# Decoder step on one core: the output projection of two prompt tiles moved between the last value products of attention, one tile left in the mixer, and evictions moved up in their steps

## The reference

```python
q_r, k_r, v_r, g_r, q_a, k_a, v_a = project(hp, w_in[i], pos_p)
ret_o, ret_fin = retention_prompt(q_r, k_r, v_r)
att_o = dilated_attention_prompt(q_a, k_a, v_a)
mix = merge_heads(ret_o, g_r, att_o, w_out[i])       # concat([retention, attention]) @ w_out, 1024 x 1024
...
h1 = layer_norm(ALPHA * h + mix, ln1_g, ln1_b)
f, conv_state = conv_ffn(h1, prefix, w_up, conv_w, conv_b, w_down)
e = jax.nn.sigmoid(h1 @ w_ple_gate) * (p @ w_ple_proj)
return layer_norm(ALPHA * h1 + f + e, ln2_g, ln2_b), conv_state
```

## Time and profile before

| | us |
|---|---|
| median of 3 runs | 1517.49 (1517.3 to 1518.66) |
| the profiled execution | 1514.99 |
| its span | 1513.2 |
| TensorE busy in the span | 1384.5 (91%) |
| VectorE busy | 798.9 (53%) |
| ScalarE busy | 462.4 (31%) |
| GpSimd busy | 273.4 (18%) |
| mean granted clock of TensorE | 0.978 of full speed |

### The profile page before, as it was taken

One profiled execution on the slowest core, in us unless ns is written; L12 is line 12 of the kernel. 1 busy time (PEld: TensorE's weight loads), 2 busy tenths in 40 slices (PEclk: granted clock), 3 DMA queues, 4 the chain that ended last, 5 costly groups with the idle time before them and its releaser, 6 DMA issues. The chain is left out here.

```text
span 1513.2 us, 23893 instructions
## 1 busy us (share of the span) xinstructions
PE 1384.5 (91%) x8896; PEld 785.1 (52%) x8896; DVE 798.9 (53%) x1601; ACT 462.4 (31%) x753; POOL 273.4 (18%) x329
## 2 busy tenths in 40 slices
PE   2699999979999858999989999999999999999986
PEld 1355555545555433344536664466654666546642
DVE  8566766637667648385524543244431445314457
ACT  3322212227566620041113442034320343202322
POOL 6301010123433306022200110001010010100117
PEclk9999999989999979999999999999999999999998
DMA  7101111027587779350024121022210122101002
GB/s 230 42 29 42 34 38 33 11 66 139 118 158 151 146 171 292 127 173 8 8 58 130 55 82 42 0 62 62 83 42 0 47 77 83 42 0 42 15 14 105
DMA packets 184493, 115.76 MB, mean 76 GB/s; under 512 B 83319, under 2 KB 168263, under 8 KB 184151
## 3 DMA queue, kind: packets, MB, share of 16 engines
q1 hardware_dynamic: 184415, 114.73, 28.8%
HBM read 85.85 MB, written 10.15 MB: 63 GB/s over the span
## 5 line engine op out<-in xcount | busy, mean ns | idle before, releaser
L1731 PE MATMUL PS<-all_HT,all_WS 128*128 128x344 f16 x3168 | 465.4, 310 | 6.6 <-POOLq L73 4.8
L1731 PEld LDWEIGHTS PS<-all_HT,all_WS 128*128 128x128 f16 x3168 | 310.5, 98 | 162.1 <-issue 8.4
L1741 PE MATMUL PS<-all_WS,ffn_HG 128*128 128x512 f16 x608 | 182.4, 379 | 3.6 <-POOL ffn_HG L1891 1.9
L461 PE MATMUL PS<-all_WS,all_HT 128*128 128x512 f16 x768 | 174.9, 386 | 6.1 <-POOLq L73 6.1
L1891 POOL TENSOR_TENSOR ffn_HG<-ffn_PRD,ffn_HG 128x1032 f32 (+1 forms) x22 | 47.2, 2145 | 653.6 <-ACT ffn_HG L1863 653.6
L1851 ACT ACTIVATE ffn_C<-PS,all_CW,all_CWS 128x1032 f32<-128x1032 f32 x44 | 53.0, 1205 | 362.0 <-PE PS L1731 362.0
L818 PE MATMUL PS<-all_WS,all_HT 128*128 128x384 f16 x768 | 132.8, 331 | 3.6 <-POOLq L73 3.6
L461 PEld LDWEIGHTS PS<-all_WS,all_HT 128*128 128x128 f16 x768 | 75.9, 99 | 96.2 <-issue 8.2
L1741 PE MATMUL PS<-ffn_WD,ffn_HG 128*128 128x512 f16 x304 | 115.3, 379 | 0.0
L818 PEld LDWEIGHTS PS<-all_WS,all_HT 128*128 128x128 f16 x768 | 73.5, 99 | 55.0 <-POOLq L73 3.9
L1741 PEld LDWEIGHTS PS<-all_WS,ffn_HG 128*128 (+1 forms) x608 | 59.4, 98 | 76.9 <-issue 6.0
(11 more groups left out here) (230 smaller groups left out, 1860.7 us busy)
## 6 DMA issues: line engine op xcount, KB each, us to landing
ffn_SU<-in_w_up SPq DMA_DIRECT2D x42, 512.0 KB, 5.0
ffn_SD<-in_w_down SPq DMA_DIRECT2D x22, 512.0 KB, 3.5
all_STG<-in_w_in SPq DMA_DIRECT2D x32, 256.0 KB, 3.4
all_STG<-in_w_in SPq DMA_DIRECT2D x32, 192.0 KB, 3.3
samples_KC<-in_cache_k_win SPq DMA_DIRECT2D x24, 256.0 KB, 4.6
all_HRES<-in_x_prompt SPq DMA_DIRECT2D x8, 512.0 KB, 8.1
out<-attention_QKV SPq DMA_DIRECT2D x64, 64.0 KB, 1.7
all_STG<-in_w_out SPq DMA_DIRECT2D x8, 512.0 KB, 4.2
```

Source lines behind the costliest of these rows:

```text
L461: mm = nc.tensor.matmul(Z(p, s)[:n], HT[:, a, k, s * P:s * P + n], WS[:, slot, b, k, :], start=(k == 0 and (a, b) == (0, 0)), stop=(k == K ...
L1731: mm = nc.tensor.matmul(U(x)[:, third], UW[:, u, a, k, x * P:(x + 1) * P], HT[:, b, k, third * T3:(third + 1) * T3], start=(k == 0 and (a, ...
L1741: mm = nc.tensor.matmul(DB[u][:rows, half], HG[:, a, l, ds(t * P, rows)], WD[b][:, l, half * 512:(half + 1) * 512], start=(l == 0 and (a, ...
```

## The change

- Retention, TensorE: in step s = 8 the product that adds up the sample parts stands ahead of the transposition of `R` instead of behind it.
- Attention, TensorE: after the values of steps 36, 37, 38 and 39 stands `mix_half(t, half)`, the output projection of tile 0 (two halves of the contraction, 24 matmuls each) and tile 1. It takes the banks of `Z` and of the first head's scores, waits for their readers, for the split chunks of w_out (4 or 8 of them) and, in the second half, for the eviction of q = 3.
- Attention, ScalarE and VectorE: `out` goes to the head of ScalarE's step, and on VectorE behind the first `mask` of the step.
- Samples: `add(0)` and `add(1)` stand first on VectorE; TensorE does tiles 2 to 5, then the halves of tile 6; nothing stands around `weigh(1)` any more. The adds in the loop move from b = 2, 4, 6 to b = 3, 5, 7.
- Mixer: `mix` of tile 7 and the sample rows only; `gate(0)` goes chunk by chunk and waits for each chunk; ScalarE and VectorE have their splits in another order around the first tile.

```diff
@@ retention, TensorE
+                            if s == NT:
+                                pe.wait_ge(zp_ready, BASE + p + 1)
+                                nc.tensor.matmul(Z(p, s)[:NB], SUMS[:], ZP[:], start=True, stop=True).then_inc(z_ready, 1)
                             q, t = tile_at(s, 4, p, kind)
                             if t is not None:
                                 pe.wait_ge(r_ready, BASE + 8 * q + t + 1)
                                 pe.wait_ge(rlo, BASE + 8 * q + t)
                                 nc.tensor.transpose(RB, R[:, t % 2], IDENT[:]).then_inc(r_turned, 1)
-                            if s == NT:
-                                pe.wait_ge(zp_ready, BASE + p + 1)
-                                nc.tensor.matmul(Z(p, s)[:NB], SUMS[:], ZP[:], start=True, stop=True).then_inc(z_ready, 1)
@@ attention, TensorE
+                    def mix_half(t, half):
+
+                        if t == 0:
+                            pe.wait_ge(copied, BASE + NG)
+                        else:
+                            pe.wait_ge(masked, BASE + 2 * NA)
+                        pe.wait_ge(w_free, BASE + 2 + 4 * (HP - 1) + 4 * half + 4)
+                        if half:
+                            pe.wait_ge(mlo, BASE + (NA - NT) // 4 + 1)
+                        for c in range(2):
+                            for k in range(4 * half, 4 * half + 4):
+                                for a, b in PASSES:
+                                    nc.tensor.matmul(M[t][:, c], MT[:, a, k, t * P:(t + 1) * P], WS[:, k // 4, b, 2 * (k % 4) + c],
+                                                     start=(k == 0 and (a, b) == (0, 0)), stop=(k == KD - 1 and (a, b) == (1, 0)))
...
                         values(g - LP)
+                        if NG <= g < NG + 4:
+                            mix_half((g - NG) // 2, (g - NG) % 2)
@@ attention, ScalarE
                     for g in range(NG + LP + 2):
+                        out(g - LP - 1)
                         soften(g)
                         copy_sum(g - 1)
                         split(g)
-                        out(g - LP - 1)
@@ samples
-        EARLY = 6
+        DRAIN, EARLY = 2, 7
...
+                    add(0)
+                    add(1)
                     nc.vector.memset(OPS[0], 0.0).then_inc(bank_zero, 1)
                     for b in range(NB):
-                        if b in (2, 4, 6):
-                            add((b - 2) // 2)
+                        if b in (3, 5, 7):
+                            add(DRAIN + (b - 3) // 2)
...
-                    for t in range(4):
+                    for t in range(DRAIN, EARLY - 1):
                         mix(t)
...
                     weigh(0)
-                    mix(5, (0,))
                     weigh(1)
-                    mix(5, (1,))
@@ mixer, TensorE, gate(0) and the head of the stage
+                            pe.wait_ge(r_ready, BASE + 2)
+                            for k in range(KD):
+                                pe.wait_ge(wlo, BASE + k + 1)
...
-                    mix(0, 0, P, EARLY * P)
-                    mix(1, 1, P, (EARLY + 1) * P)
-                    pe.wait_ge(r_ready, BASE + 1)
+                    mix_product(0, P, EARLY * P).then_inc(mixed, 1)
@@ mixer, VectorE
                     add_mix(0, 0, P, EARLY)
-                    for c in range(4, KD):
-                        split(c)
+                    split(4)
                     low(0)
-                    add_mix(1, 1, P, EARLY + 1)
+                    split(5)
+                    add_mix(1, 1, NB, NT)
+                    split(6)
+                    split(7)
                     low_p(0)
-                    add_mix(2, 0, NB, NT)
```

More of the change, by code:

```diff
@@ L1200, in _ @@
                     then(nc.vector.tensor_scalar(SR[:R8, PAT * P:], MX[:R8, 1:2], LOG3, None, ALU.add))
-                    add(3)
+                    add(5)
                     dve.wait_ge(s_turned, BASE + 1)
@@ L1212, in _ @@
                     nc.vector.memset(OPS[1], 0.0).then_inc(bank_zero, 1)
-                    add(4)
+                    add(6)
                     dve.wait_ge(summed, BASE + 1)
@@ L1233, in _ @@
                                                        ALU.add).then_inc(att_done, 1)
-                    add(5)
                     dve.wait_ge(mhi, BASE + 4)
@@ L1257, in mix @@
                     def mix(t, halves=(0, 1)):
-                        if t >= 2 and 0 in halves:
+                        if 0 in halves:
                             pe.wait_ge(r_ready, BASE + t - 1)
@@ L1283, in _ @@
                     mm.then_inc(s_turned, 1)
-                    mix(4, (0,))
+                    mix(EARLY - 1, (0,))
                     pe.wait_ge(sr_ready, BASE + 2)
@@ L1398, in gate @@
                             pe.wait_ge(sig_ready, BASE + t)
+                        else:
+                            pe.wait_ge(r_ready, BASE + 2)
+                            for k in range(KD):
+                                pe.wait_ge(wlo, BASE + k + 1)
+                                for c in range(2):
+                                    for a, b in PASSES:
+                                        mm = nc.tensor.matmul(GB[:, c], HT[:, a, k, 0:P], WG[:, b, k, c * 512:(c + 1) * 512],
+                                                              start=(k == 0 and (a, b) == (0, 0)), stop=(k == KD - 1 and (a, b) == (1, 0)))
+                            mm.then_inc(gated, 1)
+                            return
                         for c in range(2):
@@ L1484, in copy_parts @@
                         nc.scalar.activation(PP[:], src.rearrange("p b n -> p (b n)"), ACT.Copy).then_inc(pp_ready, 1)
-                    for c in range(KD):
+                    for c in range(5):
                         split(c)
-                    copy_parts(M[0], 1)
+                    copy_parts(M[1], 1)
                     high(0)
+                    for c in range(5, KD):
+                        split(c)
                     high_p(0)
```

17 lines of the change are left out of this document (5 added, 12 removed).

## The result

The changed kernel takes 1511.57 us in the median of 20 runs (1508.55 to 1518.97), against 1518.73 for the kernel before, run 20 times beside it (1517.09 to 1523.52). The ratio is 0.9952, 95% interval 0.9944 to 0.9961: 7.2 us or 0.5% faster. The forecast was 14.2 us, its range ended at 1511.0: the direction was right, the size half of what was foretold.

A forecast was written before the change was run, and what follows sets the result against it. TensorE was busy 1384.5 of 1513.2 us, so only its idle time and lower-clock matmuls could be won. Terms 4.1 + 3.6 - 6.3 + 9.9 + 2.9 = 14.2 us less gave 1503.3 us, range 1498.8 to 1511.0.

The forecast's parts named there:

- Retention, 4.1 us less: Retention seams: the sum fits into the wait for R, 0.95 us at three seams, plus 1.26 for a slow projection.
- Attention, three head pairs, 3.6 us less: Attention's head-pair seams: sooner evictions of OB save 1.2 of a 1.71 us wait at each of three.
- the prediction's own sign of being wrong: Attention: the wait for probabilities grows by what the eviction's wait lost; the other sign was halves beyond 30 us in all.
- the seams give their gain back: Rival, retention and attention: the next waits end at the old time, 7.7 us lost, 1511.0 us; chance 0.13.
- End of attention, 6.3 us more: End of attention: four halves, one behind 3.9 us of idleness at the lower clock; samples begins at 562.7 instead of 556.43.
- The barrier: Between attention's last half and the start of samples: allowed 0.4 us.
- each half tile starts cold: Rival, end of attention: every half begins at the lower clock, 4.4 us more, 1507.7 us; chance 0.16.
- Samples, 9.9 us less: Samples: 5.3 us between the weigh calls, 3.3 behind weigh(1), 1.9 from the clock staying up, less 0.6 for an add.
- The add ahead of b = 3: Samples, VectorE: free if b = 3's multiplication waits for GpSimd's; costs 1.2 us if the two merely slow each other.
- Mixer, 2.9 us less: Mixer: gate(0) may start at 662.5, after the sample add_mix, instead of 665.36; bounds 0 and 3.5 us.
- The forecast case: Whole kernel: 14.2 us less, 1503.3 us, own range 1499 to 1507; chance 0.60.
- Faster: Whole kernel: measurably faster than before, where 3.0 us tells it from no change; chance 0.91.

The follow-up runs named there:

- run 20: Not a run label but a count: the kernel before was run 20 times beside the changed kernel; median 1518.73 us.
- e2_soon: The kernel before with only the evictions of OB moved up in their steps; 1520.11 us, ratio 1.0011.
- e6_loads: The changed kernel with attention's projection-weight loads and their splits moved out of steps s = 0 and 2; 1505.51 us, ratio 0.9915.
- e9_loads_only: The kernel before with only attention's projection-weight loads and their splits moved out of steps s = 0 and 2; 1513.93 us, ratio 0.9960.
- e10_loads_late: The changed kernel with loads and splits moved, first halves before second halves, and evictions of OB back at the end of their steps; 1505.81 us, ratio 0.9900.
- e11_keys: The changed kernel with loads moved, first halves before second halves, and keys of sample rows 2 and 3 loaded ahead of the retention state; 1500.38 us, ratio 0.9860.
- e1_zsum: The kernel before with only the retention part: the sample-part sum ahead of the transposition of R; 1512.90 us, ratio 0.9955.
- e4_order: The changed kernel with first halves of both tiles before the second halves at the end of attention; 1505.15 us, ratio 0.9906.
- e5_order_late: The changed kernel with first halves before second halves and evictions of OB back at the end of their steps; 1509.02 us, ratio 0.9940.
- e7_order_loads: The changed kernel with first halves before second halves and attention's projection-weight loads and splits moved; 1499.28 us, ratio 0.9874.

## Why the prediction was wrong in size

**Retention, 4.1 us less: right, a little small.** The stage lost 4.6 us (mean of three without the edit 256.2, of eleven with it 251.6), the time 5.9. A seam gave 1.05 to 1.4 us instead of 0.95: the projection follows the transposition after 0.17 us where it took 1.21, and from the projection behind one seam to that behind the next it took 58.99 and 59.02 us instead of 60.04 and 60.45. The slow projection behind the third seam took 6.33 to 6.63 us in the three kernels without this part and 5.34 in all eleven with it. Seams and projection together gave 5.3 us, of which 0.8 is lost again between the last transposition and attention.

**Attention, three head pairs, 3.6 us less: the step that failed.** "What is late next is the transposed probabilities", I wrote, and took 1.2 of 1.71 us all the same. Measured: nothing in the time (e2_soon), and in after the waits for the eviction (5.1 us in the head pairs) came back as waits for probabilities, 10.2 us instead of 3.7: the prediction's own sign of being wrong. The stage took 200.2 to 201.4 us with late evictions and 198.5 to 204.8 with sooner ones. It was the rival "the seams give their gain back", for this half. I had given it 0.13, arguing that VectorE's work starts sooner too. It did, by 1.4 us at the first seam, but between VectorE and the values stands SyncE's queue, whose rows I had not read, and it issued the transposition no sooner (18.95 to 19.07 us into the step, with late evictions and with sooner ones, but for e2_soon). e6_loads and e9_loads_only show that loads and splits were in the way, by the profile mostly through the queue; e10_loads_late shows that moving them does not free the seams' gain: about 1.4 of the 1.78 us per seam stay lost, and how much of that is still the queue no run here separates.

**End of attention, 6.3 us more: mechanism right, 3.9 us too small.** The end took 48.1 to 49.3 us in the four kernels with this order and sooner evictions, against 38.5 to 39.0. In after, measured from the last projection's start at 518.72, the last values' half ends 45.8 us later where I had 44.3: the chunks came 1.3 us later than forecast (25.5 instead of 24.2), and a first half of 6.05 us was not fully at 2.4 GHz. The barrier I had put at 0.4 us; it takes 2.32, of which 1.68 stood in the earlier trace rows for all to read. The first product of before waited for no semaphore of its stage; now it waits for `add(0)`, and so also until GpSimd has added BASE (line 73, the releaser that the profile names). `add(0)` itself was done 0.8 us before the product began. The earlier trace rows put the fall of the clock at 541.1 rather than 541.6, which changes nothing in the sum. The rival "each half tile starts cold" did not come out: two of the four halves ran at the full clock, the first took 6.05 us behind values that ran at the lower one (30 matmuls in 1.81 us, against 1.03 in the earlier trace rows), and only the one behind 4.54 us of idleness took 7.00. The Trainium skill, TensorE: Matmul & The Clock Gate, "HAM oscillation — how this bites in real kernels", speaks of groups of matmuls that each stand behind a wait; the trace agrees for the one half that has such a wait, and the other three have none.

**Samples, 9.9 us less: right, a little small.** Means of four and of nine profiles (without e11_keys) are 84.1 and 72.6, 11.5 less; the kernel before had been profiled in an execution in which row 2's keys came 19.6 us into the stage, 2.7 and 2.9 earlier than in e1_zsum and e2_soon, so against that one profile the gain is only 9.0. Details came as foretold in after: `weigh(1)` right behind `weigh(0)`, the half behind the scores at the full clock (5.34 us), their gap 1.22 us instead of 7.28. In three changed kernels the clock fell there after all: behind 3.47 us in e4_order, 2.87 in e5_order_late and 4.59 in e11_keys that half took 7.03, 6.71 and 7.30. The add ahead of b = 3 costs nothing, by the mechanism that I had read from before. GpSimd's and VectorE's rows in after:

```profile
588.64 5.91 POOL L1178 TENSOR_TENSOR samples_SS<-samples_SS,samples_OUTER 128x2048 f32<-128x2048 f32 x1
593.01 3.15 DVE L1213 TENSOR_TENSOR samples_PRD<-samples_KC,samples_QB 128x1536 f32<-128x1536 f32 x1
```

VectorE's multiplication ends 1.61 us after GpSimd's, at 596.16 against 594.55, as it did before (585.03 against 583.42), although it began 0.95 us later against it and took 3.15 us instead of 4.10. So it waits until GpSimd's is done, and an add ahead of it on VectorE is free as long as the multiplication still begins before that.

**Mixer, 2.9 us less: 0.2.** `gate(0)` did start sooner, right behind the sample `add_mix`, but only 1.2 us. Two covers that I had not priced were gone with the tile. The chain on VectorE starts with loads, and it came later in its stage than before. This is VectorE's timeline in after, where the first `add_mix` begins 19.43 us into the stage (before 17.98, 656.06 in the earlier trace rows against the stage's start at 638.08):

```profile
650.03 0.81 DVE L1563 TENSOR_SCALAR all_HRES<-all_HRES,mixer_MV,mixer_RSTD 128x1024 f32<-128x1024 f32 x1 [1.40 <-POOL mixer_RSTD L1531]
...
659.34 1.22 DVE L1544 SCALAR_TENSOR_TENSOR all_HRES<-all_HRES,PS 128x1024 f32<-128x1024 f32 x1
...
664.80 1.20 DVE L1544 SCALAR_TENSOR_TENSOR all_HRES<-all_HRES,PS 8x1024 f32<-8x1024 f32 x1
```

And TensorE, which had worked up to `gate(0)`, now idles 5.9 us ahead of it:

```profile
656.08 1.88 PE L1437 MATMUL PS<-mixer_PP,all_SUMS 128*8 128x512 f32 x4 [0.16 <-ACT mixer_PP L1501]
663.89 1.94 PE L1395 MATMUL PS<-all_IDENT,all_HRES 128*128 128x128 f32 x8 [5.92 <-DVE all_HT L1572]
666.10 2.13 PE L1418 MATMUL PS<-mixer_WG,all_HT 128*128 128x512 f16 x7 [0.27 <-issue]
```

It pays for that with the lower clock: the eight transpositions behind the idleness take 1.94 us, those at 654.61 took 1.09, and from `gate(0)`'s start to the next transposition of `mixer_PR` it took 10.82 to 12.01 us in the ten changed kernels and 10.36 in the four with the tile. Behind that the stages are equal to 0.1 us.

**The chances.** The forecast case had 0.60 with its own range of 1499 to 1507; the median of 1511.57 lies 0.6 us above the full range. "Faster" at 0.91 was right. The terms were treated as independent, but in the changed kernel they are not: the sooner eviction's gain at the end of attention is eaten by the order of the halves. As far as the stages tell, the errors are 3.6 to 5 us (seams), 3.9 (end) and 2.7 (mixer), less 1.6 (samples) and 0.5 (retention), 8 to 9.5 in all. The gain by the medians was 7.0 us short of the forecast, so the stages of single profiles account for it only to within 1 to 3 us.

## What to carry to other kernels

Before pricing a removed wait, read the timeline of every queue between the releaser and the waiter, the one that issues transfers too; a queue without gaps gives the gain back at the next thing it issues. Where work fills a gap, order it by what each piece still needs: the same four halves cost some 5 to 6 us less when those that need only early chunks came first. And work taken out of a stage uncovers what it hid, here late loads and TensorE's clock, so price the stage anew instead of subtracting.

## What the runs showed of the hardware

- Issuing the same two transpositions (q = 7, first seam) on SyncE took 4.95 to 6.13 us in the nine kernels in which a load stands right ahead of them (6.13 in after, 5.32 in before) and 4.37 to 4.50 in the five in which it does not.
- Idleness ahead of TensorE's scores or half tile, and what the half behind it took: 0.86 to 2.77 us in seven kernels (1.22 in after, 2.31 in e7_order_loads), 5.34 each; 2.87 (e5_order_late), 6.71; 3.47 (e4_order), 7.03; 4.54 (after), 7.00; 4.59 (e11_keys), 7.30; 7.28, 6.81. The length alone does not decide it: in before, retention's projections behind 1.54 and 1.57 us of idleness took 5.35 and 6.61.
- In the fourteen profiles 42 of VectorE's multiplications of keys by queries began while one of GpSimd's 128x2048 products ran. Each ended 1.60 to 1.63 us after it, and so took up to 4.11 us; alone they take 1.76. The sums between them (line 1216 in after), which read one tensor, took 1.75 us beside such a product too.
- In all ten kernels without the mixer's second tile the third chunk of w_ple_gate was split by ScalarE 11.2 to 11.7 us into the stage, in the four with it 10.0 to 10.4, though before and after issue the loads at the same times in the stage and both move some 415 GB/s there. What delays them stays open.
- Executions differ by some us in when transfers land: in the four kernels whose code for samples is the same, the multiplication of row 2's keys began 19.6 to 22.5 us into the stage, which took 81.65 to 86.02 us.
